# A MoE encoder layer on one core: table numbers are read in one place of a step, and VectorE's step is cut elsewhere

## The chip, the cores and the metric

One NeuronCore of a Trainium2 chip runs the whole program. Five engines run side by side, each with its own instruction stream: TensorE (PE: matrix products; PEld is its weight load), VectorE (DVE), ScalarE (ACT), GpSimd (POOL) and SyncE (SP, which issues most of the transfers). They meet in semaphores only. In each engine a sequencer reads the instructions, computes addresses, takes branches and hands the work on to the engine proper; the trace has rows of a sequencer as "PEldq", "ACTq", "DVEq". The metric is the time of one execution in microseconds, the median of several runs.

## The reference, cut to what matters

One encoder layer: a token mixing part (convolution branch and chunked attention), a LayerNorm, then the part that the change touches, a mixture of 16 experts, and a second LayerNorm. Each of 1024 rows is routed to 2 of 16 experts:

```python
for e in range(N_EXPERTS):
    g, u = jnp.split(t @ w_gate_up[e], 2, axis=-1)
    out = out + combine[:, e:e + 1] * ((jax.nn.silu(g) * u) @ w_down[e])
x = layer_norm(ALPHA * x + out, ln2_g, ln2_b)
```

## The kernel before, in words

The rows are sorted by expert into tiles of 128 rows; a tile holds rows of one expert. How many tiles an expert has is known only on the chip, 21 tiles in all here. So VectorE writes a small table into SBUF (`tab`): for each tile its expert (`T_E`), the place of the expert's gate weights (`T_PAR`), the parity of the expert (`T_NEXT`), and two flags: `T_SPLIT_DN` (at this tile the down weights of the expert of the tile before are to be split) and `T_SPLIT_GU` (at this tile the gate weights of the next expert are to be split). Every engine reads the numbers that it needs into registers with `value_load`, in a step per tile (`load`, L1230). `when` reads a flag and runs its part only if the flag is set.

All products are float32 in three passes (high by high, high by low, low by high), so each operand is split into a high and a low part: ScalarE copies the high part (`gu_high`, `down_rows`, `x_t`, `h_t`), VectorE subtracts it to get the low part (`gu_low` L1329, `down_rows` L1868, `x_t` L1783, `h_t` L1872). What a step of tile i does:

- POOL gathers the 128 rows of the tile after it (`xg`) and stores the result of tile i - 2 with an adding transfer (`acc_rows`, L1367).
- PE: transposes of x (L1496), `down` of tile i - 2 (24 products, L1427 to L1429 with `dn_h`), transposes of h of tile i - 1 (L1523), `up` of tile i (48 products with `gu`). `down` and `up` read their numbers first.
- ScalarE: the high columns `xgh` (L1621), the scaled copy `ys` of tile i - 2 (L1657), the down rows `dn_h` (L1632) if flagged, `hbh` (L1638), the gate rows (L1323) if flagged, `silu` (L1648).
- VectorE: the low columns `xgl` of tile i, the late gate rows (5 to 7 of 8) of tile i - 1's flag, the down rows `dn_l` if flagged, `hbl`, the early gate rows (0 to 4) if flagged, and `hb` (the product of silu and u, L1884).
- SP loads the gate weights of expert e + 1 (4 transfers of 1 MB, L1282) when PE has used the rows that they replace, then waits until VectorE has split the down weights of the expert before and loads the next ones (2 MB, L1285). It does this in program order, by experts and not by tiles.

Steps 1 and 2 are written out. `steps` runs a loop for tiles 3 to 14 and then a nest of `If`s for tiles 15 to 30, each holding its step and all that follow; the first that fails leaves the nest (L1246). The last tile (`end1` = 20 here; `end2`, `end3` are the two before it) is written out behind the nest, in another order:

```python
        steps(pe, step, end1)
        transpose_x(end1)
        down(end3)
        transpose_h(end2)
        par = load(pe, T_PAR, end1)
        ...
        up_rows(NE - 1, bass.ds(par, 1), range(KC // 2))
        ...
        down(end2, by_row=True)
```

The result of tile `end2` is what the loads of the rows for the second LayerNorm wait for; the last tile's is added later from PSUM (`last_rows`).

Of the kernel before, what the change touches and what calls it, by code (L numbers as in the profile page):

```python
# [16 lines left out]
KC = D // P  # L17
# [11 lines left out]
NE, NGRP, EPG = 16, 4, 4  # L29
FF = 512  # L30
FC = FF // P
# [1145 lines left out]
EARLY = 5  # L1177


def moe(nc, sem, m):  # L1180
# [47 lines left out]
    def load(eng, row, i):  # L1228

        return eng.value_load(tab[0:1, row, bass.ds(i, 1)], min_val=0, max_val=NE - 1 if row == T_E else 1)  # L1230
# [5 lines left out]
        end3 = eng.value_load(ends_i[0:1, 2:3], min_val=NE - 3, max_val=MAX_TILES - 3)  # L1236
        return total, end3, end2, end1

    def steps(eng, step, end):

        with eng.Fori(3, NE - 1) as i:
            step(i)

        def from_tile(i):
            if i < MAX_TILES - 1:
                with eng.If(end > i):  # L1246
                    step(i)
                    from_tile(i + 1)
                eng.nop()
        from_tile(NE - 1)  # L1250

    def when(eng, row, i, static, then):

        if static is not None:
            if static:
                then()
            return
        flag = load(eng, row, i)
        with eng.If(flag > 0):
            then()  # L1260
        eng.nop()

    def split_gu(i):

        return True if isinstance(i, int) and i == 0 else None

    def split_dn(i):
        return {0: False, 1: True}.get(i) if isinstance(i, int) else None


    def place_of(e):

# [158 lines left out]
    def tensor_part(pe):  # L1431
# [59 lines left out]
        def transpose_x(i):  # L1491
            pe.wait_ge(gath, i * 16 + 16)
            if not (isinstance(i, int) and i == 0):
                pe.wait_ge(tx_lo, 2 * i if isinstance(i, int) else i * 2)
            for k in range(KC):
                last = pe.transpose(psf[:, P * k:P * k + P], xg[:, P * k:P * k + P], ident)  # L1496
            last.then_inc(tx_done, 1)
# [9 lines left out]
                if k % 2:  # L1507
                    last.then_inc(gu_rows, 1)

        def up(i):  # L1510

            e, par = load(pe, T_E, i), load(pe, T_PAR, i)
            pe.wait_ge(tx_lo, i * 2 + 1)
            up_rows(e, bass.ds(par, 1), range(KC // 2))
            pe.wait_ge(tx_lo, i * 2 + 2)
            up_rows(e, bass.ds(par, 1), range(KC // 2, KC))

        def transpose_h(i):
            pe.wait_ge(h_ok, i + 1)
            if not (isinstance(i, int) and i == 0):  # L1520
                pe.wait_ge(th_lo, i)
            for k in range(FC):
                last = pe.transpose(ps[:, 4, P * k:P * k + P], hb[:, P * k:P * k + P], ident)  # L1523
            last.then_inc(th_done, 1)

        def down(i, by_row=False):
            e = load(pe, T_E, i)
            pe.wait_ge(th_lo, i + 1)
            if not by_row:
                pe.wait_ge(dn_lo, e * FC + FC)  # L1530
            if not (isinstance(i, int) and i == 0):
                pe.wait_ge(y_ok, i)
            for k in range(FC):
                if by_row:
                    pe.wait_ge(dn_lo, e * FC + (k + 1))
                for h in range(2):
                    c = slice(HALF * h, HALF * h + HALF)
                    last = mm3(pe, ps[:, 6 + h, :], hbh[:, P * k:P * k + P], hbl[:, P * k:P * k + P],
                               dn_h[:, k, c], dn_l[:, k, c], k == 0, k == FC - 1)
            last.then_inc(dn_done, 1)  # L1540
# [27 lines left out]
        transpose_h(0)  # L1568
        pe.wait_ge(tx_lo, 4)
        up_rows(e, bass.ds(par, 1), range(KC // 2, KC), 2, xgh2, xgl2)  # L1570
        transpose_x(2)
        down(0)
        transpose_h(1)
        up(2)

        def step(i):
            transpose_x(i)
            down(i - 2)
            transpose_h(i - 1)
            up(i)  # L1580

        steps(pe, step, end1)
        transpose_x(end1)
        down(end3)
        transpose_h(end2)
        par = load(pe, T_PAR, end1)
        pe.wait_ge(tx_lo, end1 * 2 + 1)
        up_rows(NE - 1, bass.ds(par, 1), range(KC // 2))
        pe.wait_ge(tx_lo, end1 * 2 + 2)
        down(end2, by_row=True)  # L1590
        up_rows(NE - 1, bass.ds(par, 1), range(KC // 2, KC))
        transpose_h(end1)
        down(end1, by_row=True)


    def halves(i):
# [14 lines left out]
    def scalar_part(act):  # L1611
# [3 lines left out]
        def x_t(i):  # L1615
            act.wait_ge(tx_done, i + 1)
            if not (isinstance(i, int) and i < 2):
                act.wait_ge(gu_rows, 4 * i)
            hi = xgh2 if isinstance(i, int) and i == 1 else xgh
            for c in halves(i):  # L1620
                act.activation(hi[:, c], psf[:, c], ACT.Copy).then_inc(tx_hi, 1)  # L1621

        def down_rows(i, first=False, before=None, rows=range(FC)):
            e = 0 if first else load(act, T_E, i - 1)
            act.wait_ge(dn_in, e * 16 + 16)
            if first:

                act.wait_ge(slots_ok, 1)
            if not first:
                act.wait_ge(dn_done, i - 1 if before is None else before)  # L1630
            for k in rows:
                act.activation(dn_h[:, k, :], dn_raw[:, k, :], ACT.Copy).then_inc(dn_hi, 1)  # L1632

        def h_t(i):
# [1 line left out]
            if not (isinstance(i, int) and i == 0):  # L1636
                act.wait_ge(dn_done, i)
            act.activation(hbh[:], ps[:, 4, :], ACT.Copy).then_inc(th_hi, 1)  # L1638

        def gate_rows(i, rows):  # L1640
            e, par = load(act, T_E, i), load(act, T_NEXT, i)
            gu_high(act, e + 1, bass.ds(par, 1), rows)

        def silu(i):
            act.wait_ge(gu_rows, 4 * i + 4)
# [13 lines left out]
        def step(i):  # L1659
            first = isinstance(i, int) and i == 1  # L1660
            if not first:
                x_t(i)
            if not (isinstance(i, int) and i < 2):
                y(i - 2)
            when(act, T_SPLIT_DN, i, split_dn(i), lambda: down_rows(i, first))
            h_t(i - 1)
            when(act, T_SPLIT_GU, i, split_gu(i), lambda: gate_rows(i, range(KC)))
            silu(i)

        x_t(0)  # L1670
# [6 lines left out]
            step(i)  # L1677
        steps(act, step, end1)
        x_t(end1)
        h_t(end2)  # L1680
        y(end3)
        when(act, T_SPLIT_DN, end1, None, lambda: down_rows(end1, before=end2))
        y(end2, ys2[:], False)
        when(act, T_SPLIT_DN, total, None, lambda: down_rows(total, before=end1, rows=range(2)))
        silu(end1)
        when(act, T_SPLIT_DN, total, None, lambda: down_rows(total, before=end1, rows=range(2, FC)))
        h_t(end1)

        def total_of(t):
# [95 lines left out]
    def vector_part(dve):  # L1785
# [75 lines left out]
        dve.wait_ge(tables, 1)  # L1861
        total, end3, end2, end1 = ends(dve)

        def down_rows(i, first=False, rows=range(FC)):
            e = 0 if first else load(dve, T_E, i - 1)
            for k in rows:
                dve.wait_ge(dn_hi, e * FC + (k + 1))
                dve.tensor_tensor(dn_l[:, k, :], dn_raw[:, k, :], dn_h[:, k, :], ALU.subtract).then_inc(dn_lo, 1)  # L1868
# [2 lines left out]
            dve.wait_ge(th_hi, i + 1)  # L1871
            dve.tensor_tensor(hbl[:], ps[:, 4, :], hbh[:], ALU.subtract).then_inc(th_lo, 1)  # L1872

        def gate_rows(i, rows):
            e, par = load(dve, T_E, i), load(dve, T_NEXT, i)
            gu_low(dve, e + 1, bass.ds(par, 1), rows)

        def late_rows(i):

            when(dve, T_SPLIT_GU, i, None, lambda: gate_rows(i, range(EARLY, KC)))  # L1880

        def gate(i):
            dve.wait_ge(silu_ok, i + 1)
            dve.tensor_tensor(hb[:], hb[:], ps[:, 7 if isinstance(i, int) and i == 0 else 3, :], ALU.mult).then_inc(h_ok, 1)  # L1884

        def step(i):
            static = isinstance(i, int)
            if not (static and i == 1):
                x_t(dve, i)
                late_rows(i - 1)  # L1890
            when(dve, T_SPLIT_DN, i, split_dn(i), lambda: down_rows(i, static and i == 1))
            h_t(i - 1)
            when(dve, T_SPLIT_GU, i, None, lambda: gate_rows(i, range(EARLY)))
            gate(i)

        gu_low(dve, 1, place_of(1), range(3, 4))
        gate(0)
        gu_low(dve, 1, place_of(1), range(4, KC))
        for i in range(1, 3):
            step(i)  # L1900
        steps(dve, step, end1)
        x_t(dve, end1)
        h_t(end2)
        when(dve, T_SPLIT_DN, end1, None, lambda: down_rows(end1))
        late_rows(end2)
        dve.tensor_copy(w_last[:], w_slot[:, bass.ds(end1, 1)]).then_inc(w_set, 1)
        when(dve, T_SPLIT_DN, total, None, lambda: down_rows(total, rows=range(2)))
        gate(end1)
        when(dve, T_SPLIT_DN, total, None, lambda: down_rows(total, rows=range(2, FC - 1)))
        h_t(end1)  # L1910
        when(dve, T_SPLIT_DN, total, None, lambda: down_rows(total, rows=range(FC - 1, FC)))

        def mean(t):
            dve.wait_ge(f_tot, t + 1)
# [84 lines left out]
```

## Time and profile before

| | us |
|---|---|
| median of 3 runs | 1188.76 (1186.89 to 1188.95) |
| the profiled execution | 1186.35 |
| its span, first to last instruction | 1184.2 |
| PE busy | 1104.6 |
| DVE busy | 817.9 |
| ACT busy | 557.6 |
| mean granted TensorE clock | 0.981 |

The steps of the tiles lie between about 770 and 1150 us of the span. A busy time says that an engine worked, not that the end waited for it: that is read from the chain of waits and from the idle time ahead of a row, in brackets, with what ended it. "issue" there is time in which the engine waited for nothing that the profile shows.

### The profile page before, as it was taken

How to read it: one execution, taken by the hardware profiler on the slowest of the kernel's cores; microseconds unless marked ns; L12 is line 12 of the kernel's file. 1: busy time of each engine (PE TensorE's matmuls, PEld its weight loads, DVE VectorE, ACT ScalarE, POOL GpSimd, SP SyncE). 2: the span in 40 equal slices, each digit the busy share in tenths (PEclk: the TensorE clock that was granted, in tenths of full speed). 3: DMA queues.
4: the chain of work that ended last, by engine and by line, in shares of the span. 5: the costliest groups of instructions: out<-in, count | busy, mean ns of one | idle time of the engine just before them, and what ended most of it. 6: DMA issues, size and time to landing. Idle time of an engine off the chain costs nothing.

```text
span 1184.2 us, 17084 instructions
## 1 busy us (share of the span) xinstructions
PE 1104.6 (93%) x5645; PEld 921.6 (78%) x5646; DVE 817.9 (69%) x1147; ACT 557.6 (47%) x808; POOL 92.4 (8%) x100
## 2 busy tenths in 40 slices
PE   7999999999989989899999999989999999999970
PEld 5888888879777778778788887768788888888750
DVE  5799999835365755566586588788579556548657
ACT  5111211233476755656333033277578545548655
POOL 0000000000000000000000000044111211112220
PEclk9999999999999999999999999899999999999985
DMA  6121332322201010171334235579899866699785
GB/s 254 54 84 50 107 89 89 107 93 68 71 19 41 19 41 1 37 303 53 152 142 160 86 128 218 205 271 380 324 319 381 321 200 200 215 389 326 286 255 205
DMA packets 47862, 199.57 MB, mean 169 GB/s; under 512 B 5184, under 2 KB 5696, under 8 KB 45744
## 3 DMA queue, kind: packets, MB, share of 16 engines
q1 hardware_dynamic: 41600, 176.18, 39.4%
q0 software_dynamic: 6192, 22.48, 7.6%
q8 instruction: 41, 0.67, 0.2%
q14 instruction: 29, 0.24, 0.1%
HBM read 166.20 MB, written 32.51 MB: 168 GB/s over the span
## 4 chain that ended last, share of the span: by engine, by line
PE 76%; DMA 7%; DVE 7%; ACT 6%; issue 4%; DVEq 0%; SPq 0%; ACTq 0%; POOL 0%; POOLq 0%
PE ps L465 17%; PE ps L467 16%; PE ps L466 16%; PE ps L1427 7%; PE ps L1429 7%; PE ps L1428 7%; DMA gu<-in_wexp 5%; PE ps L550 1%; PE ps L1496 1%; PE ps L1423 1%; PE ps L536 1%; ACT pr L797 1%; ACT pth L821 1%; DVE ptl L1039 1%; DMA acc_rows<-ys,to_now 1%
## 5 line engine op out<-in xcount | busy, mean ns | idle before, releaser
L465 PE MATMUL ps<-xh,wh 128*128 128x512 f32 x512 | 203.2, 397 | 12.3 <-DVE xl L901 8.1
L467 PE MATMUL ps<-xh,wl 128*128 128x512 f32 x512 | 200.4, 391 | 0.0
L466 PE MATMUL ps<-xl,wh 128*128 128x512 f32 x512 | 200.3, 391 | 0.0
L1329 DVE TENSOR_TENSOR gu<-gu (+1 forms) x128 | 148.5, 1219 | 35.3 <-issue 23.8
L924 DVE SCALAR_TENSOR_TENSOR cv<-u,dw_t,cv 128x1024 f32<-128x1024 f32 x120 | 154.1, 1284 | 3.7
L1427 PE MATMUL ps<-gu,xgh 128*128 x336 | 133.4, 397 | 3.4 <-DVE xgl L1783 3.4
L1323 ACT ACTIVATE gu<-gu (+1 forms) x128 | 124.5, 1047 | 22.6 <-DMA gu<-in_wexp 14.5
L1429 PE MATMUL ps<-gu,xgl 128*128 x336 | 131.1, 390 | 0.0
L1428 PE MATMUL ps<-gu,xgh 128*128 x336 | 130.8, 389 | 0.0
L465 PEld LDWEIGHTS ps<-xh,wh 128*128 128x128 f32 x512 | 96.8, 189 | 34.4 <-issue 14.5
L467 PEld LDWEIGHTS ps<-xh,wl 128*128 128x128 f32 x512 | 96.7, 189 | 20.7
L466 PEld LDWEIGHTS ps<-xl,wh 128*128 128x128 f32 x512 | 96.8, 189 | 19.6 <-issue 0.5
L896 DVE TENSOR_TENSOR wl<-raw,wh 128x1024 fp32r<-128x1024 f32 x52 | 63.5, 1222 | 56.9 <-ACT wh L728 56.8
L728 ACT ACTIVATE wh<-raw 128x1024 fp32r<-128x1024 f32 x52 | 54.5, 1056 | 99.7 <-DMA raw<-in_wblk 99.5
L1868 DVE TENSOR_TENSOR dn_l<-dn_raw,dn_h 128x1024 fp32r<-128x1024 f32 x64 | 74.2, 1218 | 11.4 <-ACT dn_h L1632 10.6
L1039 DVE TENSOR_TENSOR ptl<-ps,pth 128x512 fp32r<-128x512 f32 (+1 forms) x72 | 41.0, 596 | 57.2 <-ACT pth L821 57.2
L1427 PEld LDWEIGHTS ps<-gu,xgh 128*128 128x128 f32 x336 | 63.1, 188 | 17.2 <-issue 5.0
L1429 PEld LDWEIGHTS ps<-gu,xgl 128*128 128x128 f32 x336 | 63.1, 188 | 13.5
L1428 PEld LDWEIGHTS ps<-gu,xgh 128*128 128x128 f32 x336 | 63.2, 188 | 12.5
L1427 PE MATMUL ps<-dn_h,hbh 128*128 128x512 f32 x168 | 68.4, 407 | 3.3 <-DVE hbl L1872 3.3
L1632 ACT ACTIVATE dn_h<-dn_raw 128x1024 fp32r<-128x1024 f32 x64 | 62.6, 1048 | 8.5 <-DMA dn_raw<-in_wexp 5.1
L1428 PE MATMUL ps<-dn_l,hbh 128*128 128x512 f32 x168 | 66.5, 396 | 0.0
(259 smaller groups left out, 2053.0 us busy)
## 6 DMA issues: line engine op xcount, KB each, us to landing
gu<-in_wexp SPq DMA_DIRECT2D x64, 1024.0 KB, 8.8
dn_raw<-in_wexp SPq DMA_DIRECT2D x16, 2048.0 KB, 11.0
raw<-in_wblk SPq DMA_DIRECT2D x52, 512.0 KB, 4.0
gate_cols<-gst SPq DMA_DIRECT2D x16, 512.0 KB, 5.2
xraw<-in_xT SPq DMA_DIRECT2D x8, 512.0 KB, 7.7
gcm<-gate_cols SPq DMA_DIRECT2D x8, 512.0 KB, 7.0
gam<-gate_cols SPq DMA_DIRECT2D x8, 512.0 KB, 15.0
x<-in_x SPq DMA_DIRECT2D x8, 512.0 KB, 5.7
```

Of the source, the lines that this page charges most:

```text
L465: pe.matmul(o, a_h, b_h, start=first, stop=False)
L466: pe.matmul(o, a_h, b_l, start=False, stop=False)
L467: return pe.matmul(o, a_l, b_h, start=False, stop=last)
L896: dve.tensor_tensor(lo, src, hi, ALU.subtract).then_inc(w_lo, 1)
L924: dve.scalar_tensor_tensor(out=cv[:, j, :], in0=tap, scalar=w, in1=cv[:, j, :], op0=ALU.mult, op1=ALU.add).then_inc(conv_d, 1)
L1323: eng.activation(gu[:, par, k, 0, :], gu[:, par, k, 1, :].bitcast(F32), ACT.Copy).then_inc(gu_hi, 1)
L1329: eng.tensor_tensor(gu[:, par, k, 1, :], gu[:, par, k, 1, :].bitcast(F32), gu[:, par, k, 0, :], ALU.subtract).then_inc(gu_lo, 1)
L1427: pe.matmul(o, a_h, b_h, start=first, stop=False)
L1428: pe.matmul(o, a_h, b_l, start=False, stop=False)
L1429: return pe.matmul(o, a_l, b_h, start=False, stop=last)
L1632: act.activation(dn_h[:, k, :], dn_raw[:, k, :], ACT.Copy).then_inc(dn_hi, 1)
L1868: dve.tensor_tensor(dn_l[:, k, :], dn_raw[:, k, :], dn_h[:, k, :], ALU.subtract).then_inc(dn_lo, 1)
```

## The change

All engines run the same instructions on the same data. On PE the three numbers of a step (expert of the tile of `down`, expert and place of the tile of `up`) are read ahead of the transposes of x, in the written-out last tile too, behind the nest. On ScalarE the five numbers are read behind the columns and ahead of `ys`. On VectorE the step of tile i now begins with the reads and the down rows and ends with the columns of tile i + 1 and the late rows, whose flag and numbers are those of the same step; its loop covers tiles 3 to 13, its nest 14 to `end2` - 1, and `end2` is written out behind it. `when` becomes `given`, which gets the flag instead of reading it.

```diff
@@ steps
-    def steps(eng, step, end):
-        with eng.Fori(3, NE - 1) as i:
+    def steps(eng, step, end, least=NE - 1):
+        with eng.Fori(3, least) as i:
             step(i)
...
-        from_tile(NE - 1)
-    def when(eng, row, i, static, then):
-        if static is not None:
-            if static:
-                then()
+        from_tile(least)
+    def given(eng, flag, then):
+        if flag is None:
+            then()
             return
-        flag = load(eng, row, i)
         with eng.If(flag > 0):
             then()
         eng.nop()
...
+    def weights_of(eng, i):
+        if isinstance(i, int) and i == 1:
+            return None, 0, load(eng, T_SPLIT_GU, 1), load(eng, T_E, 1), load(eng, T_NEXT, 1)
+        return (load(eng, T_SPLIT_DN, i), load(eng, T_E, i - 1), load(eng, T_SPLIT_GU, i), load(eng, T_E, i),
+                load(eng, T_NEXT, i))
@@ PE
-        def up(i):
-            e, par = load(pe, T_E, i), load(pe, T_PAR, i)
+        def up(i, e, par):
...
-        def down(i, by_row=False):
-            e = load(pe, T_E, i)
+        def down(i, e, by_row=False):
...
         def step(i):
+            e_down = 0 if isinstance(i, int) and i == 2 else load(pe, T_E, i - 2)
+            e, par = load(pe, T_E, i), load(pe, T_PAR, i)
             transpose_x(i)
-            down(i - 2)
+            down(i - 2, e_down)
             transpose_h(i - 1)
-            up(i)
+            up(i, e, par)
...
         steps(pe, step, end1)
+        e_3, e_2, par = load(pe, T_E, end3), load(pe, T_E, end2), load(pe, T_PAR, end1)
         transpose_x(end1)
-        down(end3)
+        down(end3, e_3)
         transpose_h(end2)
-        par = load(pe, T_PAR, end1)
@@ ScalarE
             if not first:
                 x_t(i)
+            begun, e_down, begins, e, par = weights_of(act, i)
             if not (isinstance(i, int) and i < 2):
                 y(i - 2)
-            when(act, T_SPLIT_DN, i, split_dn(i), lambda: down_rows(i, first))
+            given(act, begun, lambda: down_rows(i, e_down, first))
             h_t(i - 1)
-            when(act, T_SPLIT_GU, i, split_gu(i), lambda: gate_rows(i, range(KC)))
+            given(act, begins, lambda: gu_high(act, e + 1, bass.ds(par, 1), range(KC)))
             silu(i)
...
         x_t(end1)
+        begun, e_down, last_begun = load(act, T_SPLIT_DN, end1), load(act, T_E, end2), load(act, T_SPLIT_DN, total)
         h_t(end2)
@@ VectorE
+        def half_step(i):
+            begun, e_down, begins, e, par = weights_of(dve, i)
+            given(dve, begun, lambda: down_rows(e_down))
+            h_t(i - 1)
+            given(dve, begins, lambda: gu_low(dve, e + 1, bass.ds(par, 1), range(EARLY)))
+            gate(i)
+            x_t(dve, i + 1)
+            def late_rows():
+                given(dve, begins, lambda: gu_low(dve, e + 1, bass.ds(par, 1), range(EARLY, KC)))
+            return late_rows
         def step(i):
-            static = isinstance(i, int)
-            if not (static and i == 1):
-                x_t(dve, i)
-                late_rows(i - 1)
-            when(dve, T_SPLIT_DN, i, split_dn(i), lambda: down_rows(i, static and i == 1))
-            h_t(i - 1)
-            when(dve, T_SPLIT_GU, i, None, lambda: gate_rows(i, range(EARLY)))
-            gate(i)
+            half_step(i)()
...
-        steps(dve, step, end1)
-        x_t(dve, end1)
+        steps(dve, step, end2, NE - 2)
+        late_rows = half_step(end2)
+        begun, e_down, last_begun = load(dve, T_SPLIT_DN, end1), load(dve, T_E, end2), load(dve, T_SPLIT_DN, total)
         h_t(end2)
-        when(dve, T_SPLIT_DN, end1, None, lambda: down_rows(end1))
-        late_rows(end2)
+        given(dve, begun, lambda: down_rows(e_down))
+        late_rows()
```

## Rows read from the trace of the kernel before

**Rows 1.** The page: busy time, share of the span, instructions.
```profile
...
PE 1104.6 (93%) x5645; PEld 921.6 (78%) x5646; DVE 817.9 (69%) x1147; ACT 557.6 (47%) x808; POOL 92.4 (8%) x100
...
```

**Rows 2.** Busy time by stretch: PE, PEld, DVE, ACT, POOL (x), PEclk, DMA share, GB/s.
```profile
...
790.00:830.00 40.00, 38.70 (x183) 31.73 (x182) 36.72 (x36) 28.08 (x34) 21.39 (x10) 1.00 1.02 388
830.00:835.00 5.00, 2.59 (x13) 1.74 (x12) 1.92 (x4) 4.17 (x6) 0.02 (x1) 1.00 0.74 311
835.00:1111.00 276.00, 276.00 (x1307) 229.66 (x1307) 187.31 (x190) 172.57 (x205) 52.27 (x61) 1.00 0.85 301
1111.00:1122.00 11.00, 8.31 (x41) 6.42 (x40) 5.71 (x7) 4.97 (x7) 1.50 (x1) 1.00 0.57 233
...
```

**Rows 3.** Chain of waits, 840 to 1076 us: start, us, what.
```profile
...
845.96 0.87 PE ps L1496 x8
...
1058.44 0.87 PE ps L1496 x8
...
```

**Rows 4.** Chain of waits, 1111 to 1146 us.
```profile
...
1121.47 0.49 PE ps L1427
...
1132.43 0.24 PE ps L1429
...
1134.68 9.54 DMA acc_rows<-ys,to_now
...
```

**Rows 5.** Timeline, 832 to 835.2 us: start, us, engine, line, work [idle before].
```profile
...
832.22 0.69 DVE L1884 TENSOR_TENSOR hb<-hb,ps 128x512 f32<-128x512 f32 x1 [2.19 <-ACT hb L1648]
832.83 1.28 DVE L1783 TENSOR_TENSOR xgl<-ps,xgh 128x512 fp32r<-128x512 f32 x2
...
832.97 0.66 PE L1523 MATMUL ps<-ident_t,hb 128*128 128x128 f32 x4 [1.23 <-DVE hb L1884]
...
834.80 0.49 PE L1427 MATMUL ps<-gu,xgh 128*128 x1 [1.18 <-DVE xgl L1783]
...
```

**Rows 6.** Line 1230 in 832.9 to 834.6 us: xcount, ns min/median/max, first to last start.
```profile
...
L1230 PEldq FUSED_REGOPS  x4: 37/101/151, 833.0 to 834.2; - x4
...
L1230 DVEq TENSOR_LOAD <-tab x2: 302/309/316, 833.3 to 834.1; - x2
L1230 PEldq SEQ_ASSERT  x2: 18/18/18, 833.7 to 834.4; - x2
...
```

**Rows 7.** Line 1246, the branches of the nest, whole run.
```profile
...
L1246 PEldq COMPARE_BRANCH  x6: 68/80/6073, 1019.0 to 1107.3; - x6
L1246 ACTq COMPARE_BRANCH  x6: 34/34/50, 1023.2 to 1114.1; - x6
L1246 DVEq COMPARE_BRANCH  x6: 43/43/63, 1023.9 to 1116.4; - x6
...
```

**Rows 8.** Timeline of PE, 1111 to 1121.8 us.
```profile
...
1111.17 0.39 PE L1429 MATMUL ps<-gu,xgl 128*128 x1
1113.67 1.09 PE L1496 MATMUL ps<-ident_t,xg 128*128 128x128 f32 x8 [2.11 <-issue]
...
1120.29 0.60 PE L1523 MATMUL ps<-ident_t,hb 128*128 128x128 f32 x4
...
```

**Rows 9.** Chain of waits, 1111 to 1146 us, ScalarE's part.
```profile
...
1119.84 0.04 ACTq L1616
...
```

**Rows 10.** Timeline of DVE, 1096.9 to 1121.9 us.
```profile
...
1097.15 0.69 DVE L1884 TENSOR_TENSOR hb<-hb,ps 128x512 f32<-128x512 f32 x1 [0.57 <-ACT hb L1648]
...
1100.43 3.50 DVE L1329 TENSOR_TENSOR gu<-gu  x3 [1.39 <-issue]
...
```

**Rows 11.** Timeline of DVE, 786 to 811 us.
```profile
...
799.48 4.62 DVE L1868 TENSOR_TENSOR dn_l<-dn_raw,dn_h 128x1024 fp32r<-128x1024 f32 x4
...
```

**Rows 12.** Line 1782, first instruction behind DVE's nest.
```profile
...
L1782 DVEq FUSED_REGOPS  x1: 53/53/53, 1119.2 to 1119.2; - x1
...
```

**Rows 13.** Waits, 700 to 1184 us: total, times, longest.
```profile
...
ACT ys L1657 <- PE ps L1429: 64.8, 17, 4.9
...
```

**Rows 14.** Line 1230, whole run.
```profile
...
L1230 PEldq TENSOR_LOAD <-tab x60: 295/302/330, 772.7 to 1142.3; - x60
...
```

More of the change, by code:

```diff
@@ L1261, in when @@
         eng.nop()
[L1263 to L1268, printed above, removed]
+    def weights_of(eng, i):
[3 more added lines that the diff above has]
+                load(eng, T_NEXT, i))
     def place_of(e):
@@ L1570, in tensor_part @@
         up_rows(e, bass.ds(par, 1), range(KC // 2, KC), 2, xgh2, xgl2)
[L1571 to L1574, printed above, removed]
         def step(i):
+            e_down = 0 if isinstance(i, int) and i == 2 else load(pe, T_E, i - 2)
+            e, par = load(pe, T_E, i), load(pe, T_PAR, i)
             transpose_x(i)
-            down(i - 2)
+            down(i - 2, e_down)
             transpose_h(i - 1)
-            up(i)
+            up(i, e, par)
+        step(2)
         steps(pe, step, end1)
+        e_3, e_2, par = load(pe, T_E, end3), load(pe, T_E, end2), load(pe, T_PAR, end1)
         transpose_x(end1)
-        down(end3)
+        down(end3, e_3)
         transpose_h(end2)
-        par = load(pe, T_PAR, end1)
         pe.wait_ge(tx_lo, end1 * 2 + 1)
@@ L1589, in tensor_part @@
         pe.wait_ge(tx_lo, end1 * 2 + 2)
-        down(end2, by_row=True)
+        down(end2, e_2, by_row=True)
         up_rows(NE - 1, bass.ds(par, 1), range(KC // 2, KC))
         transpose_h(end1)
-        down(end1, by_row=True)
+        down(end1, NE - 1, by_row=True)
     def halves(i):
@@ L1621, in x_t, with down_rows @@
                 act.activation(hi[:, c], psf[:, c], ACT.Copy).then_inc(tx_hi, 1)
-        def down_rows(i, first=False, before=None, rows=range(FC)):
-            e = 0 if first else load(act, T_E, i - 1)
+        def down_rows(i, e, first=False, before=None, rows=range(FC)):
             act.wait_ge(dn_in, e * 16 + 16)
@@ L1638, in h_t @@
             act.activation(hbh[:], ps[:, 4, :], ACT.Copy).then_inc(th_hi, 1)
-        def gate_rows(i, rows):
-            e, par = load(act, T_E, i), load(act, T_NEXT, i)
-            gu_high(act, e + 1, bass.ds(par, 1), rows)
         def silu(i):
@@ L1679, in scalar_part @@
         x_t(end1)
+        begun, e_down, last_begun = load(act, T_SPLIT_DN, end1), load(act, T_E, end2), load(act, T_SPLIT_DN, total)
         h_t(end2)
         y(end3)
-        when(act, T_SPLIT_DN, end1, None, lambda: down_rows(end1, before=end2))
+        given(act, begun, lambda: down_rows(end1, e_down, before=end2))
         y(end2, ys2[:], False)
-        when(act, T_SPLIT_DN, total, None, lambda: down_rows(total, before=end1, rows=range(2)))
+        given(act, last_begun, lambda: down_rows(total, NE - 1, before=end1, rows=range(2)))
         silu(end1)
-        when(act, T_SPLIT_DN, total, None, lambda: down_rows(total, before=end1, rows=range(2, FC)))
+        given(act, last_begun, lambda: down_rows(total, NE - 1, before=end1, rows=range(2, FC)))
         h_t(end1)
@@ L1862, in vector_part, with down_rows @@
         total, end3, end2, end1 = ends(dve)
-        def down_rows(i, first=False, rows=range(FC)):
-            e = 0 if first else load(dve, T_E, i - 1)
+        def down_rows(e, rows=range(FC)):
             for k in rows:
@@ L1872, in h_t @@
             dve.tensor_tensor(hbl[:], ps[:, 4, :], hbh[:], ALU.subtract).then_inc(th_lo, 1)
[L1874 to L1880, printed above, removed]
         def gate(i):
@@ L1900, in vector_part @@
             step(i)
-        steps(dve, step, end1)
-        x_t(dve, end1)
+        steps(dve, step, end2, NE - 2)
+        late_rows = half_step(end2)
+        begun, e_down, last_begun = load(dve, T_SPLIT_DN, end1), load(dve, T_E, end2), load(dve, T_SPLIT_DN, total)
         h_t(end2)
-        when(dve, T_SPLIT_DN, end1, None, lambda: down_rows(end1))
-        late_rows(end2)
+        given(dve, begun, lambda: down_rows(e_down))
+        late_rows()
         dve.tensor_copy(w_last[:], w_slot[:, bass.ds(end1, 1)]).then_inc(w_set, 1)
-        when(dve, T_SPLIT_DN, total, None, lambda: down_rows(total, rows=range(2)))
+        given(dve, last_begun, lambda: down_rows(NE - 1, range(2)))
         gate(end1)
-        when(dve, T_SPLIT_DN, total, None, lambda: down_rows(total, rows=range(2, FC - 1)))
+        given(dve, last_begun, lambda: down_rows(NE - 1, range(2, FC - 1)))
         h_t(end1)
-        when(dve, T_SPLIT_DN, total, None, lambda: down_rows(total, rows=range(FC - 1, FC)))
+        given(dve, last_begun, lambda: down_rows(NE - 1, range(FC - 1, FC)))
         def mean(t):
```

## The prediction

> **What bounds the kernel now.** I read the page's head first: TensorE (PE) is busy in 93% of the span [rows 1]. Then the busy time of the stretches from 790 us on, where the changed code runs [rows 2]: between 835 and 1111 us PE is busy for 276.00 of 276 us. Nothing that another engine does in there is worth anything as long as PE is fed. The chain of waits shows the same: the transposes that open each tile's step follow each other every 17.71 us, thirteen in a row from 845.96 to 1058.44 us [rows 3].
>
> So time can be won or lost in three places. (1) 790 to 835 us: the DMA share is 1.02 at 388 GB/s, the transfers are the limit, and PE stands still for 2.4 of the last 5 us. (2) 1111 to 1122 us: PE is busy for 8.31 of 11 us. (3) The start of the last run of products that the end waits for: 48 products from 1121.47 to 1132.67 us, then a copy by ScalarE and the adding store of 9.54 us, then the loads and the last LayerNorm [rows 4]. Nothing behind 1132.67 is touched, so the end moves with the start of that run.
>
> **The change, part by part.** A read of a table number is a load of 0.30 us with an address computation and a check around it. On PE two reads run from 832.97 to about 834.5 us, so one costs 0.76 us; two on VectorE stand 0.8 us apart [rows 6]. They are done by the engine's sequencer, which runs ahead of the engine. How far ahead on PE: its branch at the last step starts at 1107.3 us, while the array finishes what was issued before it at 1111.40 us [rows 7, 8], a lead of 4.0 us.
>
> *PE in a full step.* Before, one read lies behind the transposes of x and two behind the transposes of h; now three lie ahead of the transposes of x. 3 x 0.76 = 2.3 us out of 4.0 (some 3.6 where the loop turns, by a branch of a few tenths): **0**. The cover is the queue of products already issued; 1.3 us of it are left, and without it each of 17 steps would pay.
>
> *PE where it had run dry, near 833 us.* It had waited for VectorE's `hb` (832.22 + 0.69). Four transposes, then the two reads, then the products at 834.80: idle for 1.18 us [rows 5]. Their first operand `xgl` was there at 832.83 + 0.68 = 833.51. Without the reads the products start 0.3 us behind it (that is what lies between the last read and the first product now), at 833.8: **-1.0 us**, and the saturated stretch moves by it. Bounds: -1.2 (the transposes' own end decides) and -0.7 (both halves of `xgl` are wanted). The same reads ahead of tile 2's products, in the stretch in which the transfers are the limit, also go, but there PE only comes earlier to its wait for `hb`, which hangs on a transfer. I take 0 for it.
>
> *PE behind the last step.* When the tiles end, the branch at L1246 leaves a nest of ten steps that aren't run. It takes 6.07 us on PE, the five branches before it 0.07 to 0.08 us [rows 7]. The array is dry at 1111.40 and gets its transposes at 1113.67, after 2.11 us of "issue" [rows 8]. The lead is used up, so the three reads that now stand between branch and transposes are paid in full: **+2.3 us**. Part of that is hidden: PE ends its transposes of h at 1120.29 + 0.44 = 1120.73 but starts the products at 1121.47, since ScalarE, whose own branch began at 1114.1, came to its next instruction at 1119.84 only [rows 7, 9]. ScalarE is 1.0 us earlier after the change, like all behind 835 us, so it gives way: -0.7. The start of the last products moves by -1.0 + 2.3 - 0.7 = **+0.6 us**.
>
> The Trainium skill (Runtime: NRT & Kernel Launch, Instruction fetch mechanics) says that a taken branch to outside a window of two blocks makes the sequencer fetch its target by DMA before it goes on. The trace agrees so far that only the branch that leaves the nest is long. By that rule the reads neither shorten nor lengthen a jump, and VectorE's comes at another time.
>
> *VectorE's step.* The order of its work is the same (gate, next columns, late rows, down rows, h, early rows); the loop is cut elsewhere. Eight reads, three of them ahead of the late rows, become five ahead of the down rows. The hole of 1.39 us ahead of the late rows [rows 10] closes; the five reads, 4.0 us, lie behind three rows of 1.14 us already issued, so at most 0.6 us of it is given back. Where VectorE decides when the transfers start (to 804 us) it has no hole [rows 11], and in the saturated stretch it feeds PE in time as it is. **0**.
>
> *VectorE's jump, one tile earlier.* It leaves its nest at tile 19, not 20. Before, the branch began at 1116.4 and the next instruction came at 1119.2 [rows 7, 12], 2.9 us beside a wait for ScalarE. Now it follows the issue of the late rows of tile 18, about 1098.2 - 1.0 = 1097.2 us by the work at 1097.15 [rows 10], amid full transfers. Price: between those 2.9 us and PE's 6.07; ScalarE's 5.8 us also lay among transfers, so I take 5.8. Then 1097.2 + 5.8 + 4.0 of reads = 1107.0; four down rows and `hbl` to 1112.2; five early rows to 1117.9; `hb` at 1118.5. PE wants `hb` at 1120.29 - 1.0 + 2.3 = 1121.6: slack 3.1 us, so **0** up to a jump of 8.9 us. Behind VectorE waits SP, whose load of the next down weights then goes out some 3 us later.
>
> *ScalarE.* Five reads stand together between the columns and the copy `ys`, in place of beside the later work. `ys` waits for PE 17 times, 64.8 us in all, 3.8 us each [rows 13], and five reads of 0.76 take 3.8: **0**, with at most a few tenths on a copy that nothing wants soon. SP and POOL issue what they issued.
>
> **Sum:** +0.6 us. The profiled execution took 1186.35 us, becoming 1186.9; the median of the runs shown lies 2.4 us above it, so 1189.3 us. A difference can be told from no change here from about 0.2%, 2.4 us.
>
> **The rivals.**
> *A. The jumps get cheaper (faster).* VectorE's delay moves SP's next load back, so there may be less in the queues when PE jumps. With 2.9 us for PE in place of 6.07 the transposes are at 1113.67 - 1.0 + 2.3 - 3.2 = 1111.8, ScalarE decides, and the products start 1.0 us earlier than before: 1187.8. If ScalarE's jump shortens by as much, 2.6 us earlier: 1186.1. For: the two long jumps lay amid transfers, the short one at 1116 behind them. Against: the gate weights are on their way at 1107 in any case.
>
> *B. VectorE's early jump holds PE (slower).* Place: `hb` of tile 19. It decides from 8.9 us. If the block behind the target is wanted too, two times 5.8 = 11.6 us, `hb` is 2.7 us late on top of the 0.6: 1192.1.
> The section named above speaks for this one: it calls runtime control flow expensive for such fetches, and gives no time for one beside full queues.
>
> *C. PE's lead isn't enough (slower).* If three reads and the branch outlast it by 0.5 us, 17 steps pay 8.5 us: 1197.8. It decides from reads of 1.2 us in place of 0.76. Against: over 60 loads on PE the range is 0.295 to 0.330 us [rows 14].
>
> *D. The change doesn't do what it could near 833 us*, because `hb` or `xgl` come later by as much: +1.6 us, 1190.4.
>
> **How the numbers follow.** Forecast 0.55, A 0.17, B 0.10, C 0.05, D 0.13. Half of A, half of B and all of C lie beyond 0.2%, and a bit of the forecast on either side, since the three runs shown spread over 2.1 us by themselves: faster 0.17, same 0.64, slower 0.19. The range for 8 in 10 goes from A with both jumps short, 1186.0, to B, 1192.2.
>
> **What would show it.** PE's transposes stay 17.71 us apart (else C). Near 833 us the products start about 0.8 us after the transposes of h, not 1.8. At the last step PE's branch is long again and the transposes follow its end by 2.3 us. VectorE shows a long jump near 1098 us and no hole ahead of its late rows. The forecast is wrong if PE's jump changes its length by more than 2 us, or if PE waits for `hb` or `hbl` between 1111 and 1122 us.

## The result and the profile after

The changed kernel took 1189.89 us (median of 20 runs, 1186.11 to 1192.86), the kernel before 1187.44 us in 20 runs on the same chip. The ratio is 1.0021, with a 95% interval of 1.0012 to 1.0030: slower by 2.5 us, just beyond what a measurement can tell from no change. A ratio with its interval, here and below, rests on all runs of both kernels and need not be the quotient of the two medians. The profiled execution took 1192.52 us, its span is 1190.4 us, 6.2 us longer than the one of before.

The page's head after the change, and the stretches from 790 us on (PE, PEld, DVE, ACT, POOL busy, then PEclk, DMA share, GB/s):

```profile
PE 1110.6 (93%) x5645; PEld 927.4 (78%) x5646; DVE 817.2 (69%) x1147; ACT 555.7 (47%) x808; POOL 95.9 (8%) x100
```

```profile
790.00:830.00 40.00, 38.42 (x179) 31.57 (x180) 37.52 (x38) 26.75 (x33) 23.24 (x9) 1.00 1.00 370
830.00:836.00 6.00, 3.87 (x19) 2.98 (x17) 2.77 (x5) 5.14 (x7) 1.42 (x3) 0.95 0.96 406
836.00:1109.00 273.00, 273.00 (x1289) 226.95 (x1289) 180.11 (x184) 168.34 (x202) 54.30 (x61) 0.99 0.85 300
1109.00:1123.00 14.00, 9.60 (x40) 7.84 (x39) 9.55 (x9) 7.85 (x10) 1.17 (x1) 0.88 0.71 233
```

PE has as many instructions as before but is busy for 6.0 us more [rows 1]. That isn't more work: the granted clock is below 1.00 in three of the four stretches, where it was 1.00 in all of them [rows 2], and ahead of them, between 731 and 757 us, PE has 20.5 us at half speed in this profile and 10.2 us in the one of before. From 790 to 1140 us the record of the clock has two stretches of 3.4 us at half speed, the lower of its two levels (1.2 GHz), from 835.4 us and from 1118.7 us. Between 836 and 1109 us PE is never idle, as before. The chain of waits has the transposes of x in the same steps, 17.71 us apart:

```profile
848.52 0.87 PE ps L1493 x8
...
1061.01 0.87 PE ps L1493 x8
```

The timeline near 833 us (all engines, other rows left out):

```profile
834.58 0.69 DVE L1864 TENSOR_TENSOR hb<-hb,ps 128x512 f32<-128x512 f32 x1 [2.40 <-ACT hb L1635]
835.18 1.28 DVE L1772 TENSOR_TENSOR xgl<-ps,xgh 128x512 fp32r<-128x512 f32 x2
...
835.32 1.08 PE L1518 MATMUL ps<-ident_t,hb 128*128 128x128 f32 x4 [2.13 <-DVE hb L1864]
...
836.11 0.79 PE L1424 MATMUL ps<-gu,xgh 128*128 x1
```

The products start 0.79 us behind the transposes, where it was 1.83 us with a hole of 1.18 us [rows 5]. Their durations (1.08 us in place of 0.66, 0.79 in place of 0.49) are those of the lower clock.

The end of the nest. First the branches of L1246, then the reads of L1230 from 1100 us on, PE's part (x, ns min/median/max, first to last start):

```profile
L1246 DVEq COMPARE_BRANCH  x6: 43/50/63, 1010.4 to 1101.6; - x6
...
L1246 PEldq COMPARE_BRANCH  x6: 68/77/6119, 1021.6 to 1109.9; - x6
L1246 ACTq COMPARE_BRANCH  x6: 34/34/50, 1025.8 to 1118.3; - x6
```

```profile
L1230 PEldq FUSED_REGOPS  x6: 37/101/151, 1116.1 to 1118.1; - x6
L1230 PEldq TENSOR_LOAD <-tab x3: 302/303/313, 1116.2 to 1117.7; - x3
```

And the timelines of PE and of VectorE there:

```profile
1113.74 0.39 PE L1426 MATMUL ps<-gu,xgl 128*128 x1
1118.53 1.84 PE L1493 MATMUL ps<-ident_t,xg 128*128 128x128 f32 x8 [4.40 <-issue]
...
1126.55 0.60 PE L1518 MATMUL ps<-ident_t,hb 128*128 128x128 f32 x4
1126.91 0.48 PE L1424 MATMUL ps<-gu,xgh 128*128 x1
```

```profile
1101.50 3.49 DVE L1326 TENSOR_TENSOR gu<-gu  x3
1113.45 4.63 DVE L1856 TENSOR_TENSOR dn_l<-dn_raw,dn_h 128x1024 fp32r<-128x1024 f32 x4 [8.46 <-issue]
1118.00 0.68 DVE L1860 TENSOR_TENSOR hbl<-ps,hbh 128x512 fp32r<-128x512 f32 x1
1118.60 5.75 DVE L1326 TENSOR_TENSOR gu<-gu  x5
1124.27 0.68 DVE L1864 TENSOR_TENSOR hb<-hb,ps 128x512 f32<-128x512 f32 x1
```

PE's jump is as long as before (6.12 and 6.07 us [rows 7]) and the standstill is 4.40 us, not 2.11 [rows 8]: the three reads stand between 1116.1 and the transposes at 1118.53, and nothing covers them. On VectorE a hole of 8.46 us is new. Its branch at 1101.6 is followed by the first read at 1107.1.

Put side by side, the start of one and the same instruction in the two profiled executions:

| | before | after | later by |
|---|---|---|---|
| a product of PE ahead of its changed code | 773.01 | 775.19 | 2.18 |
| tile 2's first product | 796.52 | 797.98 | 1.46 |
| first product behind `hb`, near 833 | 834.80 | 836.11 | 1.31 |
| transposes of x, next step (from the chain) | 845.96 | 848.52 | 2.56 |
| last product ahead of the standstill | 1111.17 | 1113.74 | 2.57 |
| transposes of x of the last tile | 1113.67 | 1118.53 | 4.86 |
| transposes of h | 1120.29 | 1126.55 | 6.26 |
| first of the last products | 1121.47 | 1126.91 | 5.44 |
| the adding store | 1134.68 | 1140.09 | 5.41 |

The 2.2 us at the top are no part of the change. They come with the stretches at half clock between 731 and 757 us: these last 10.2 us in six of the fourteen profiles of this study and 17.1 or 20.5 us in the other eight, and the two profiles of the kernel before differ in their place. The 3.2 us that are left at the store are -0.9 up to the first product behind `hb` (-0.7 of it at tile 2), +1.3 and +1.4 for the two stretches at half clock, +2.3 for the reads behind the jump, and -0.8 for the hole that waited for ScalarE [rows 9]. Without the clock's 2.7 us that is +0.6. The store, from the chain of waits, then takes 10.62 us in place of 9.54 [rows 4]:

```profile
1140.09 10.62 DMA acc_rows<-ys,to_now
```

### The profile page after: what moved, and what is told of

Its sections match the earlier page's. It is cut to its first block, busy times and chain, and to the rows that moved or that the text cites. A ratio compares the mean times of both kernels' runs of the same rounds, so it can differ in the third digit from the quotient of the medians.

```text
span 1190.4 us, 16962 instructions
## 1 busy us (share of the span) xinstructions
PE 1110.6 (93%) x5645; PEld 927.4 (78%) x5646; DVE 817.2 (69%) x1147; ACT 555.7 (47%) x808; POOL 95.9 (8%) x100
## 4 chain that ended last, share of the span: by engine, by line
PE 80%; DVE 5%; ACT 5%; DMA 5%; issue 3%; SPq 0%; ACTq 0%; POOL 0%; DVEq 0%; POOLq 0%
PE ps L465 17%; PE ps L467 16%; PE ps L466 16%; PE ps L1424 8%; PE ps L1426 8%; PE ps L1425 8%; DMA gu<-in_wexp 3%; PE ps L1493 1%; PE ps L1420 1%; PE ps L550 1%; PE ps L536 1%; ACT pr L797 1%; ACT pth L821 1%; DMA acc_rows<-ys,to_now 1%; DVE ptl L1039 1%
## 5 line engine op out<-in xcount | busy, mean ns | idle before, releaser
L1426 PE MATMUL ps<-dn_h,hbl 128*128 128x512 f32 x168 | 66.7, 397 | 0.0
```

The lines of the kernel that those rows point to most:

```text
L1426: return pe.matmul(o, a_l, b_h, start=False, stop=last)
```

## The experiments

Each ran five rounds beside the kernel before. The first three take one engine's part alone into the old kernel.

**TensorE's part alone.** In the old kernel, only PE's code of the diff.

> The kernel before with PE's part of the change alone: its reads together ahead of the transposes of x, in every step and behind the nest; ScalarE and VectorE as before. Theory P (the loss is PE's own: three reads behind the jump out of the nest, 2.3 us, and a slow clock behind longer standstills): as slow as the whole change, +1.5 to +3 us against before; the transposes behind the nest follow the end of PE's branch by 2.3 to 2.4 us. Rival V (VectorE's jump one tile earlier holds PE or SP): 0, between -1 and +1 us. Rival S (ScalarE's reads ahead of ys): 0.

Measured: 1187.97 us, 1.0017 (1.0006 to 1.0029). The transposes of the last tile follow 4.35 us of issue, and both half-clock stretches, at 834.0 and 1117.3 us, are there. That is +2.0 us, within the range expected by theory P. The reads behind the jump cost what they cost in the changed kernel, and without VectorE's part the time is much the same.

**VectorE's part alone.**

> The kernel before with VectorE's part alone: its step turned, five reads in one place, nest left one tile earlier. Theory P: 0, between -1 and +1 us, though VectorE's down rows at tile 19 come some 5 to 9 us later than before, since the jump takes 5 to 6 us there and a second stop may stand among the reads. Rival V: +1.5 to +3 us, with PE waiting for hb or hbl between 1111 and 1125 us. Rival S: 0.

Measured: 1190.05 us, 1.0026 (1.0017 to 1.0035), as much as the whole change: +3.1 us, where theory P said 0 and rival V +1.5 to +3. PE's timeline, then VectorE's:

```profile
1116.98 1.09 PE L1512 MATMUL ps<-ident_t,xg 128*128 128x128 f32 x8 [2.18 <-issue]
1119.64 0.47 PE L1443 MATMUL ps<-dn_h,hbh 128*128 128x512 f32 x1 [1.56 <-DVE hbl L1887]
```

```profile
1114.16 4.63 DVE L1883 TENSOR_TENSOR dn_l<-dn_raw,dn_h 128x1024 fp32r<-128x1024 f32 x4 [8.53 <-issue]
1118.71 0.69 DVE L1887 TENSOR_TENSOR hbl<-ps,hbh 128x512 fp32r<-128x512 f32 x1
```

PE's own standstill is the old one of 2.18 us, and a new one of 1.56 us stands behind it, for VectorE's `hbl`, followed by 3.4 us at half clock (from 1120.1 us). In the changed kernel this wait can't be seen, since PE is 2.3 us late itself.

**ScalarE's part alone.**

> The kernel before with ScalarE's part alone: five reads between the columns and ys. Theory P and rival V: 0, between -1 and +1 us. Rival S (ys and with it the down rows come later and hold PE or the store): +1.5 to +3 us.

Measured: 1187.81 us, 1.0009 (1.0000 to 1.0018). No new wait of PE shows in its trace. At most it is a small loss, for which no row stands.

**The changed kernel with PE's last reads in their old places.**

```diff
-        e_3, e_2, par = load(pe, T_E, end3), load(pe, T_E, end2), load(pe, T_PAR, end1)
         transpose_x(end1)
-        down(end3, e_3)
+        down(end3, load(pe, T_E, end3))
         transpose_h(end2)
+        par = load(pe, T_PAR, end1)
...
-        down(end2, e_2, by_row=True)
+        down(end2, load(pe, T_E, end2), by_row=True)
```

> The changed kernel with one part undone: behind the nest PE reads its three numbers where it did before (behind the transposes of x, behind the transposes of h, ahead of the second down). Theory P: 2.3 us less than the changed kernel, so -0.8 to +0.8 us against before. Rival V: as slow as the whole change, +1.5 to +3 us.

Measured: 1189.24 us, 1.0019 (1.0009 to 1.0029), not to be told from the changed kernel's 1.0021. Theory P had -0.8 to +0.8 us here and missed; PE's timeline says why:

```profile
1114.96 1.61 PE L1493 MATMUL ps<-ident_t,xg 128*128 128x128 f32 x8 [2.29 <-issue]
1117.56 0.77 PE L1424 MATMUL ps<-dn_h,hbh 128*128 128x512 f32 x1 [0.99 <-DVE hbl L1860]
```

The standstill is back at 2.29 us, and VectorE's `hbl` takes the place of the reads. The two losses lie beside each other, and removing one uncovers the other. The clock is at half for 6.8 us from 1115.4 us on.

**The changed kernel with the last tiles' numbers read ahead of the nest, on all three engines.** The jumps stay where they are, VectorE's one tile earlier.

```diff
@@ PE
+        e_3, e_2, par_last = load(pe, T_E, end3), load(pe, T_E, end2), load(pe, T_PAR, end1)
         step(2)
         steps(pe, step, end1)
-        e_3, e_2, par = load(pe, T_E, end3), load(pe, T_E, end2), load(pe, T_PAR, end1)
@@ VectorE (ScalarE's three reads move likewise)
+        of_end2 = weights_of(dve, end2)
+        begun, e_down, last_begun = load(dve, T_SPLIT_DN, end1), load(dve, T_E, end2), load(dve, T_SPLIT_DN, total)
...
-        late_rows = half_step(end2)
-        begun, e_down, last_begun = load(dve, T_SPLIT_DN, end1), load(dve, T_E, end2), load(dve, T_SPLIT_DN, total)
+        late_rows = half_step(end2, of_end2)
```

> The changed kernel with every number of the last two tiles read ahead of the nest, on PE, ScalarE and VectorE, so that nothing is read behind a jump; the jumps stay, VectorE's one tile earlier. Theory P+V (the loss is the reads behind the jumps: 2.3 us on PE, and on VectorE five reads with a second stop among them that bring hbl late): PE's transposes follow its branch at once, VectorE's down rows of tile 19 start 4 to 7 us earlier than in the changed kernel, and the time is 2 to 3.5 us below the changed kernel, -1 to +1 us against before. Rival J (VectorE's jump itself, not the reads): PE waits for hbl for some 1 us, +1 to +2 us against before. Rival K (the clock behind PE's longer standstill near 833 us alone): +2 to +3 us against before, as the changed kernel.

Measured: 1186.10 us, 0.9993 (0.9979 to 1.0006). The timelines of PE and VectorE:

```profile
1112.99 1.09 PE L1493 MATMUL ps<-ident_t,xg 128*128 128x128 f32 x8 [2.06 <-issue]
```

```profile
1104.04 4.63 DVE L1856 TENSOR_TENSOR dn_l<-dn_raw,dn_h 128x1024 fp32r<-128x1024 f32 x4 [2.46 <-ACT dn_h L1623]
1108.59 0.68 DVE L1860 TENSOR_TENSOR hbl<-ps,hbh 128x512 fp32r<-128x512 f32 x1
```

VectorE's down rows start 9.4 us earlier than in the changed kernel, 3.2 us of which are the shift of the whole run. Its hole is 2.46 us now and ends with a wait for ScalarE, so its early jump is hidden, with nothing for PE to wait for. What the reads behind the jumps cost together, with what the clock does behind them, is the difference to the changed kernel: 1.0021 - 0.9993 = 0.28%, or 3.3 us, give or take 1.9 us by the two intervals. Rivals J and K, a loss of +1 us or more, are out.

**The changed kernel without the nest**, its tiles run by a loop whose bound is a register, so that no engine leaves a nest; **the kernel before with the same loop**; and **the kernel before once more** as a control.

```diff
-        with eng.Fori(3, least) as i:
+        with eng.Fori(3, end) as i:
             step(i)
...
-        from_tile(least)
```

> The changed kernel with a loop up to the tile count read on the chip, in place of the fixed loop and the nest, on all engines that have a nest; no far jump is left, the tail lies right behind the loop. Theory P+V: PE's 6.1 us branch and VectorE's 5.5 us jump with its second stop vanish, PE never stands between 1105 and 1125 us, 4.5 to 7 us below the changed kernel, -2 to -4.5 us against before. If the long branches are not jumps to code that isn't there yet but the work of leaving the nest's levels, the same. If the time behind the branch comes from the transfers alone, any branch there stays long and the time is that of the changed kernel.

> The kernel before with the same loop in place of its nest. Theory P+V: PE's 2.1 us of standstill at 1111 us goes, and ScalarE's 5.8 us jump too: -2 to -4 us against before. Beside the other one it says what the change is worth where no engine jumps: the changed kernel with a loop is then within 1 us of this one, a little faster if the 1.0 us near 833 us counts, slower if the clock takes it back.

> The kernel before, unchanged, as one more kernel: what a difference of nothing looks like. Ratio 1.000 with its interval across it; mean clocks from 0.975 to 0.981 as in the runs of before; the profile shows the standstill at 1111 us and its branch of about 6 us again, and a slow clock of 10 to 20 us in all between 730 and 757 us.

Measured: 1182.42 us, 0.9950 (0.9930 to 0.9970, 6 runs; the medians of the two kernels give 0.9959); 1185.08 us, 0.9977 (0.9967 to 0.9987); the control 1187.74 us, 1.0002 (0.9991 to 1.0012). The changed kernel with the loop, PE and VectorE:

```profile
1114.02 0.39 PE L1418 MATMUL ps<-gu,xgl 128*128 x1
1114.25 1.03 PE L1485 MATMUL ps<-ident_t,xg 128*128 128x128 f32 x8
```

```profile
1105.37 4.63 DVE L1848 TENSOR_TENSOR dn_l<-dn_raw,dn_h 128x1024 fp32r<-128x1024 f32 x4 [1.03 <-ACT dn_h L1615]
```

PE goes on 0.23 us behind its last product, the spacing of any two. The three reads are there as before, and now they are under the queue of issued products. The nest cost the kernel before 2.7 us and the changed one 8.4 us (0.9950 against 1.0021; 7.4 us with 0.9959), both jumps and reads together. With no jump the change is worth 0.9950 - 0.9977 = -0.27%, some -3 us (the medians lie 2.7 us apart), which the two intervals leave between about -0.05 and -0.5%. This version beats both kernels. It gave more than was expected in both: 4.5 to 7 us against the changed kernel, and at most 1 us or so between the two loops. The 1.0 us near 833 us is a part of that difference, and what the rest is stays open. The control shows that the clock falls without the change too: the same kernel as before has, in its profiled execution, two stretches that the first one did not have (PEclk is the third number from the right):

```profile
834.00:837.40 3.40, 3.40 (x10) 2.66 (x9) 3.22 (x3) 3.40 (x5) 0.98 (x1) 0.51 0.60 76
1113.90:1117.30 3.40, 3.40 (x13) 2.98 (x12) 0.94 (x1) 2.87 (x4) 0.98 (x1) 0.50 0.90 379
```

**The loop with PE's part alone, and with VectorE's part alone.** These are the first two experiments with the edit above.

> The kernel before with TensorE's part of the change alone, and every engine's tiles run by a loop with a bound in a register, so that nothing jumps out of a nest. The old kernel with such a loop took 0.9977 of the kernel before (-2.7 us), the changed one 0.9950 (-5.9 us). Theory of the reads behind the jumps: TensorE's part cost +2.0 us in the nest since its three reads stood behind the jump; here they are covered, and its gain near 833 us (1.0 us by the standstill of 1.18 us) stays. It is at 0.9968 +- 0.0012, with TensorE without a gap over 0.5 us between 1100 and 1114 us. Rival, that TensorE's part is itself costly (its reads ahead of the transposes make it come late at each stop): 0.998 or more. Rival, that it carries the whole gain of the change in a loop: 0.9950.

> The kernel before with VectorE's part alone, all tiles in the loop as well. Theory of the reads behind the jumps: VectorE's part cost +3.1 us in the nest since five reads and a second stop stood behind its jump; here nothing is late and it is the old kernel with the loop, 0.9977, or less by what the closed hole ahead of the late rows gives near the end: 0.9965 +- 0.0015, with hbl of the last tile but one before 1110 us. Rival, that five reads in one place make VectorE late in every form: 0.999 or more, and TensorE waits for hbl or hb for over 0.5 us near 1112 us.

Measured: 1183.87 us, 0.9968 (0.9955 to 0.9981), and 1184.21 us, 0.9974 (0.9961 to 0.9986, 8 runs). Against the old kernel with the loop that is -0.09% and -0.03%, both within the noise: the parts lost 0.17% and 0.26% with the nest, and neither loses without it. PE has no gap over 0.3 us between 1100 and 1114 us in either. Both ratios are inside the expected ranges; their sum is less than the whole change gives in a loop (-0.27%), by no more than the intervals allow.

**VectorE's part alone, its numbers read ahead of the nest.** The second experiment, with VectorE's lines of the fifth.

> VectorE's part alone in the nest, as in the run that took 1.0026 of the kernel before, with the numbers of the last two tiles read ahead of the nest; VectorE's jump stays one tile earlier. Theory: the reads behind the jump and the second stop among them are what held TensorE for hbl. hbl comes near 1110 us in place of 1118.7, TensorE's wait for it is gone, and the kernel is at 1.0000 +- 0.0010. Rival, that VectorE's earlier jump costs time itself: the wait for hbl stays at 1 us or more and the kernel is at 1.002 or more.

Measured: 1188.56 us, 1.0014 (1.0001 to 1.0027). VectorE's timeline:

```profile
1102.01 3.48 DVE L1345 TENSOR_TENSOR gu<-gu  x3
1107.93 4.63 DVE L1883 TENSOR_TENSOR dn_l<-dn_raw,dn_h 128x1024 fp32r<-128x1024 f32 x4 [2.44 <-ACT dn_h L1648]
1112.48 0.69 DVE L1887 TENSOR_TENSOR hbl<-ps,hbh 128x512 fp32r<-128x512 f32 x1
```

`hbl` comes 6.2 us earlier than with the reads behind the jump (2.5 us later than I had written), and PE's wait for it is gone, as the theory has it. The time fell by about half of the loss only, and the interval covers both sides. Here the theory explains the row and not the whole of the number: the profile has two stretches at half clock near 792 and 836 us, and none behind PE's standstill.

**PE's three reads behind the nest made twice**, the results the same.

```diff
         e_3, e_2, par = load(pe, T_E, end3), load(pe, T_E, end2), load(pe, T_PAR, end1)
+        e_3, e_2, par = load(pe, T_E, end3), load(pe, T_E, end2), load(pe, T_PAR, end1)
```

> The changed kernel with TensorE's three reads behind its nest made twice, the computation unchanged. Theory: what stands behind TensorE's jump is paid in full: the transposes come 2.3 us later (6.7 us of issue in place of 4.4), and since TensorE alone is late there by now, the end moves by 2.3 us as well: 1.0040 +- 0.0015 of the kernel before, against 1.0021 of the changed one. Rival, that other engines' lateness (VectorE's hbl, ScalarE) hides a part: +0.5 to +1.5 us, 1.0025 to 1.0034. Rival, that a standstill longer than 3 us costs a second stretch at half clock: +4 us or more, 1.0055.

Measured: 1191.09 us, 1.0035 (1.0022 to 1.0048), within the expected range and 1.7 us above the changed kernel, though the two intervals overlap; the reading rests on the row. PE's timeline, and the stretch behind it:

```profile
1109.99 0.39 PE L1426 MATMUL ps<-gu,xgl 128*128 x1
1116.81 1.97 PE L1493 MATMUL ps<-ident_t,xg 128*128 128x128 f32 x8 [6.42 <-issue]
```

```profile
1112.40:1122.60 10.20, 5.79 (x18) 4.95 (x19) 9.96 (x11) 3.57 (x5) 0.80 (x1) 0.50 0.56 210
```

The standstill grows by 2.0 us for three more reads, about their full price, and here the clock is at half for 10.2 us, from the middle of the standstill on, so that more than one stretch at half clock did come, at less than the +4 us that the rival had put on it.

## Why the prediction was right in its steps and low in its sum

The forecast was 1189.3 us, the median came out at 1189.89, inside the range. Part of that nearness is luck: the forecast carried the median of the three runs shown, 1188.76, and the kernel before took 1187.44 in the runs beside the changed one. The effect was +0.6 predicted and +2.5 measured. In the two profiles the steps that the prediction priced do add up to +0.6; what it had put at nothing, without a reason, is the clock.

*PE in a full step, 0: right.* It is 17.71 us from transposes to transposes, with three reads ahead of them. Rival C is out.

*PE near 833 us, -1.0: right.* `hb` was 2.36 us later than before in the two profiled executions and PE's products 1.31 us later, so the products gained 1.05 us on it. Tile 2's reads gave 0.7 us at 797 us, and PE handed it back in a longer wait for `hb` (2.13 us, not 1.23), as the prediction said when it took 0. Rival D is out.

*PE behind the last step, +2.3, less 0.7 of ScalarE: right*, with +2.3 and -0.8. PE's part alone and the doubled reads show the same price by themselves.

*The jumps.* PE's took 6.12 us; rival A's cheaper jumps did not come. What does make the kernel faster is to have no jump at all, which no rival held. One reading behind rival A was rough: ScalarE's jump of 5.8 us began amid transfers at 1114.1 us, but the DMA share was 0.18 from 1117 us and 0.03 from 1118 us on, beside VectorE's jump of 2.9 us.

*VectorE's jump one tile earlier: the 0 held in the changed kernel, the terms behind it did not.* The jump was as sized, 5.5 us from branch to next instruction against 5.8. Three other things were not. It began at 1101.6 us, not 1097.2: 3.6 us of that are the shift of the whole run (2.6 later in place of 1.0 earlier), and 0.8 are its own. The reads behind it weren't 4.0 us but 6.3: the fourth stops for over 2 us, between the end of one register operation at 1110.1 and the next entry at 1112.5. Line 1230 on VectorE, 1101 to 1110 us and then 1110 to 1113.4 us:

```profile
L1230 DVEq FUSED_REGOPS  x8: 53/128/190, 1107.1 to 1109.9; - x8
```

```profile
L1230 DVEq SEQ_ASSERT  x2: 23/23/23, 1112.5 to 1113.2; - x2
```

Then, the slack was worked out for `hb` alone, while PE met `hbl` first: VectorE had finished it at 1118.7 us in the changed kernel, and PE could take it at 1120.0 only because its own reads had made it 2.3 us late. So PE waits for neither product there, and 1.3 us are left of the slack. Where PE isn't late, the step does cost: 1.56 us of waiting in VectorE's part alone, 0.99 us with PE's reads moved back. And the sum has to take the larger of the two engines' losses and not both: 3.1 us for VectorE's part, 2.0 for PE's, 2.5 for both. Rival B had the engine and the second stop right, and named the wrong product (`hb`, not `hbl`) and a threshold that was too high.

What stands in the stops can be seen among the transfers. The queues that bring instructions are named in the trace. For the time of VectorE's second stop, 1110.1 to 1112.5 us:

```profile
q14 instruction: 1, 0.01, 0.8%
```

This transfer of 8 KB runs from 1110.8 to 1111.1 us, and VectorE goes on 1.4 us behind it. Its jump has another, over at 1105.5 us, 1.6 us ahead of the first read, and PE's jump has one of 16 KB, over at 1114.6 us, 1.5 us ahead of PE's first read. The second stop lies between the same two instructions in the four profiles in which VectorE reads five numbers there, and each time it holds such a transfer. In the kernels with the loop there is none at all from 1000 to 1114 us. The trace doesn't say for which engine a transfer came, so that the second stop is another fetch for VectorE is argued from its place in time, though well supported. Nor does it say what fills the 3.7 us from the start of PE's branch to the start of the transfer.

The Trainium skill (Runtime: NRT & Kernel Launch, Instruction fetch mechanics) says that a taken branch out of the window stalls for a fetch and names this as a reason why runtime control flow is expensive. The traces agree where a nest is left (6.1 us on PE, 5.5 us on VectorE, with a transfer of instructions in each). The loop, whose branch back costs PE no gap, shows that the runtime bound is not what is paid. That the distance of the target is, and not the number of levels left, fits the transfers but was not tested by itself.

*The clock, which the prediction left out: this is the term that failed.* It worked from an execution with no half-clock stretch between 760 and 1140 us and priced none; the two stretches of the changed kernel's profile cost 1.3 and 1.4 us. But the runs of every kernel spread by the clock. Of the changed kernel's 20 runs, 11 have a mean granted clock of 0.973 or 0.974 and take 1191.4 us on average, and 9 have 0.978 or 0.979 and take 1187.1 us. The kernel before has both kinds too: of its 94 runs beside the experiments, 34 are at 0.978 or above, with 1185.9 us on average, and 60 below, with 1187.8 us. So among runs of high clock the change costs 1.2 us, and among those of low clock 3.6 us. The low ones aren't more frequent (11 of 20 against 60 of 94); they are lower, by about what one or two more stretches of 3.4 us make.

The profiles show one place where such stretches come in. Behind PE's last standstill, between 1112 and 1123 us, PE is at half clock in all five kernels in which it stands longer behind the nest or waits for `hbl`; in two of the other five profiles with a nest (the control and the fifth experiment); and in none of the four with the loop. Over all runs, a mean clock of 0.975 or below is found in 35 of 66 in those five kernels, in 7 of 72 in the seven others but one, and in 9 of the 94 of the kernel before. The exception is the eleventh experiment, without either, with 6 of 12. This mean also holds the stretches between 731 and 757 us. So a longer standstill goes with a lower clock, and that is enough to make of +0.6 us of work the +2.5 that was measured; the runs do not isolate it, and the exception says that something else lowers the clock too. How the 2.5 us divide between the two stays open, and with it about half of the price of VectorE's part.

## What to carry to other kernels

A branch out of a nest of written-out steps is a point at which an engine loses its lead: what is placed directly behind it is paid in full, here 0.76 us for each number read on PE, while the same reads in the loop or ahead of the nest had no cost that could be told from nothing. Price such an edit by every product that the engine hands on behind the jump, the first one too, and compare the engines with each other rather than adding their losses. Before arranging work around such a jump, try the loop with the bound in a register: it gave 0.23% to the kernel before and 0.7% to the changed one, which ends 0.5% below the kernel before.

## What the runs showed of the hardware beyond that

Whether the clock falls behind a standstill of PE can't be read from its length alone. In the first profile of the kernel before, PE goes on at full clock after 2.11 us of issue at 1113.67 us [rows 8]; in the control, after 2.10 us at the same place, it is at half from 1113.9 us. Near 836 us it fell behind waits for `hb` in some profiles and not in others, whichever kernel ran. With 6.4 us of standstill it fell before PE went on, at 1112.4 us, and PE's first 5.8 us of work were at half speed. By my estimate from these 5.8 us that costs some 2.9 us in one place, more than the 2.3 us of the three reads themselves.
